# Modulation strips moved into the four rounds without routes of the PEER value product, and a new order of VectorE's work in banded attention

## What is computed

```python
mod = c_act @ mod_w[l] + mod_b[l]            # 6 vectors of 1024: shift, scale, gate, twice
sh1, sc1, g1, sh2, sc2, g2 = jnp.split(mod, 6, axis=-1)
x = x + g1 * mixer(modulate(x, norm_g[l, 0], sh1, sc1))
x = x + g2 * peer(modulate(x, norm_g[l, 1], sh2, sc2), ...)
# peer: scores -> top 16 experts e and softmax weights g for each head; then
a = gelu(einsum('pd,phkd->phk', xb, u_tab[e]))
y = einsum('phk,phkd->pd', g * a, v_tab[e])
```

## Time and profile before

| | |
|---|---|
| median of 3 runs | 2687.52 us |
| the profiled execution | 2687.45 us, its span 2685.8 us |
| TensorE matmuls busy | 2580.2 us (96%) |
| VectorE busy | 2113.9 us (79%) |
| ScalarE, GpSimd busy | 1215.1 us (45%), 461.2 us (17%) |
| mean granted TensorE clock | 0.98 |
| HBM read | 531.85 MB, 199 GB/s over the span |

### The profile page before, as it was taken

One profiled execution on the slowest core, in us unless ns is written; L12 is line 12 of the kernel. 1 busy time (PEld: TensorE's weight loads), 2 busy tenths in 40 slices (PEclk: granted clock), 3 DMA queues, 4 the chain that ended last, 5 costly groups with the idle time before them and its releaser, 6 DMA issues.

```text
span 2685.8 us, 49507 instructions
## 1 busy us (share of the span) xinstructions
PE 2580.2 (96%) x17564; PEld 2253.9 (84%) x17564; DVE 2113.9 (79%) x3580; ACT 1215.1 (45%) x1760; POOL 461.2 (17%) x365
## 2 busy tenths in 40 slices
PE   5999999999999999899999999999999999999998
PEld 4879999888877877799998888778888799767986
DVE  6787997887898768867978888998777877657754
ACT  3444444554434445444444554434445454324543
POOL 1104992000000100006990000000011000100000
PEclk8999999999999999899999999999999999999999
DMA  8655555454567877354555555567786556854454
GB/s 310 249 187 159 178 176 172 163 168 161 170 214 230 286 251 249 123 175 160 177 176 172 164 165 167 187 225 261 263 281 249 191 190 200 294 206 163 158 183 146
DMA packets 147628, 536.92 MB, mean 200 GB/s; under 512 B 16784, under 2 KB 17168, under 8 KB 147232
## 3 DMA queue, kind: packets, MB, share of 16 engines
q1 hardware_dynamic: 115088, 417.08, 46.5%
q0 software_dynamic: 31104, 113.26, 12.3%
q10 hardware_dynamic: 1296, 4.72, 0.5%
HBM read 531.85 MB, written 3.15 MB: 199 GB/s over the span
## 4 chain that ended last, share of the span: by engine, by line
PE 78%; DVE 9%; issue 4%; POOL 3%; DMA 2%; ACT 2%; DVEq 0%; ACTq 0%; SPq 0%; POOLq 0%
PE ps L1933 20%; PE ps L1504 9%; PE ps L2646 7%; PE ps L716 6%; PE ps L1478 6%; PE ps L1430 5%; PE ps L1508 5%; PE ps L2628 4%; PE ps L1482 3%; POOL split_lo L1555 3%; PE ps L1891 3%; PE ps L2632 2%; DVE split_lo L1567 2%; DMA ring<-in_stream 1%; PE ps L369 1%
## 5 line engine op out<-in xcount | busy, mean ns | idle before, releaser
L1542 ACT ACTIVATE split_hi<-ring 128x1024 fp32r<-128x1024 f32 x764 | 805.3, 1056 | 773.5 <-PE ps L1482 202.3
L1567 DVE TENSOR_TENSOR split_lo<-ring,split_hi 128x1024 fp32r<-128x1024 f32 x576 | 703.2, 1221 | 202.5 <-ACT split_hi L1542 201.9
L1555 POOL TENSOR_TENSOR split_lo<-ring,split_hi 128x1024 fp32r<-128x1024 f32 x128 | 342.7, 2695 | 155.6 <-ACT split_hi L1542 155.2
L1539 ACT ACTIVATE gate_hi<-gate 128x256 fp32r x256 | 106.9, 418 | 442.3 <-PE ps L1933 442.3
L1933 PE MATMUL ps<-split_hi,gate_hi 128*128 128x512 f32 x1024 | 285.9, 400 | 1.0 <-ACT split_hi L1542 0.5
L1933 PE MATMUL ps<-split_hi,gate_lo 128*128 128x512 f32 x1024 | 277.8, 392 | 1.8 <-DVE gate_lo L1565 1.7
L1933 PE MATMUL ps<-split_lo,gate_hi 128*128 128x512 f32 x1024 | 276.8, 391 | 0.0
L1478 PE MATMUL ps<-h_parts,split_hi 128*128 128x256 f32 x2048 | 266.8, 283 | 0.0
L1504 PE MATMUL ps<-h_parts,split_hi 128*128 128x512 f32 x1024 | 261.2, 397 | 0.0
L1478 PEld LDWEIGHTS ps<-h_parts,split_hi 128*128 128x128 f32 x2048 | 254.9, 192 | 0.0
L386 POOL DMA_DIRECT2D mod_w<-in_mod x96 | 51.0, 531 | 1141.4 <-ACT gate L1608 418.3
(11 more groups left out here) (399 smaller groups left out, 4018.3 us busy)
## 6 DMA issues: line engine op xcount, KB each, us to landing
ring<-in_stream SPq DMA_DIRECT2D x782, 512.0 KB, 4.3
mod_w<-in_mod POOLq DMA_DIRECT2D x96, 512.0 KB, 4.8
small<-in_mod POOLq DMA_DIRECT2D x80, 512.0 KB, 5.8
gate<-in_mod POOLq DMA_DIRECT2D x32, 512.0 KB, 7.0
gate<-in_mod ACTq DMA_DIRECT2D x8, 512.0 KB, 11.6
gate<-in_mod SPq DMA_DIRECT2D x8, 512.0 KB, 10.2
x_kept<-x POOLq DMA_DIRECT2D x4, 512.0 KB, 3.6
gate<-x_kept POOLq DMA_DIRECT2D x4, 512.0 KB, 8.2
```

Source lines behind the costliest of these rows:

```text
L1542: nc.scalar.activation(split_hi[:, e, :], ring[:, slot, e * D:(e + 1) * D], ACT.Copy).then_inc(hi_made, 1)
L1555: nc.gpsimd.tensor_tensor(split_lo[:, e, :], ring[:, slot, e * D:(e + 1) * D], split_hi[:, e, :].bitcast(F32), ALU.subtract).then_inc(lo_m ...
L1567: nc.vector.tensor_tensor(split_lo[:, e, :], ring[:, (START[name] + j) % RING, e * D:(e + 1) * D], split_hi[:, e, :].bitcast(F32), ALU.sub ...
```

## The change

Three parts. First, in both layers' v products the six strips are made in rounds 4 to 7 only: four slabs with two chunks each, then one slab with none, in which TensorE sums; the store is one slab later. (Every 16th slab has neither.) For that, rounds 4 to 6 are written out on VectorE and TensorE. Second, x is copied to HBM as four DMAs of 256 KB, each issued when its half is ready. Third, the order of VectorE's work in banded attention. The core of the diff:

```diff
@@ peer_score_scalar
-            a.wait_ge(x_kept, 32 * (l + 1))
+            a.wait_ge(x_kept, 64 * (l + 1))
@@
-        STRIP_CHUNKS = [[0], [1], [2], [3, 4], [5], [6], [7], []]
+        STRIP_SUMS, STRIP_STORES = (4, 9, 14, 20, 25, 30), (5, 10, 15, 21, 26, 31)
@@ routed_slab_vector
-            if odd and with_strip:
-                strip_part_vector(v, l, i, j)
@@ strip_part_vector
-            for k in STRIP_CHUNKS[j]:
-                strip_chunk_vector(v, l, i * DC - 2 * DC, k, 8 * l)
-            if j == 7:
-                strip_store_vector(v, l, i - 2)
+            q, k = divmod(8 * (i - 4) + j - (8 * (i - 4) + j) // 16, 5)
+            if 8 * (i - 4) + j in STRIP_STORES:
+                strip_store_vector(v, l, STRIP_STORES.index(8 * (i - 4) + j))
+            if (8 * (i - 4) + j) % 16 < 15 and k < 4:
+                for n in (2 * k, 2 * k + 1):
+                    strip_chunk_vector(v, l, q * DC, n, 8 * l)
@@ peer_routes_vector
-            with v.eng.Fori(4, 7) as i:
+            for i in range(4, 7):
                 for j in range(8):
                     slab(i, j)
@@ peer_out_tensor, body
-                    if j == 7 and strip:
-                        strip_sum(t, i * DC + (before - DC))
+                    if strip and 8 * (i - 4) + j in STRIP_SUMS:
+                        strip_sum(t, before + DC * (STRIP_SUMS.index(8 * (i - 4) + j) + 1))
@@
-            for i0, i1, routes, strip in ((1, 2, True, False), (2, 4, True, True), (4, 7, False, True)):
+            for i0, i1, routes, strip in ((1, 2, True, False), (2, 4, True, False)):
                 with t.eng.Fori(i0, i1) as i:
                     body(i, routes, strip)
             t.seen.clear()
+            for i in range(4, 7):
+                body(i, False, True)
@@ softmax_vector(..., ahead=4)
-            for i, part in ((0, 0), (0, 1), (1, 0), (1, 1)):
+            parts = [(0, 0), (0, 1), (1, 0), (1, 1)]
+            for i, part in parts[:ahead]:
                 logits(i, part)
                 maxima(i, part)
             probT_vector(v, at_, 0)
+            for i, part in parts[ahead:]:
+                logits(i, part)
+                maxima(i, part)
@@ swa_vector
-            row_from_col(v, "g1_1", modc[:, PLACE[MOD1[1] + G1], :], 5, "V")
             for b in range(5, 8):
                 less_splits_vector(v, "swa_q", b, b + 1)
                 side_chunks_vector(v, "swa", b - 1, b)
-            side_chunks_vector(v, "swa", 7, 9)
+            row_from_col(v, "g1_1", modc[:, PLACE[MOD1[1] + G1], :], 5, "V")
+            side_chunks_vector(v, "swa", 7, 8)
+            turned_vector(v, "swa_k", kT_s, bank=4, chunks=2)
             ... (rotation of the queries)
-            turned_vector(v, "swa_k", kT_s, bank=4, chunks=2)
             turned_vector(v, "swa_qt", qT_s, bank=4)
             softmax_vector(...
-                           [lambda: None,
+                           [lambda: side_chunks_vector(v, "swa", 8, 9),
             ...
+                           ahead=3)
@@ gpsimd
-                    pool.dma_start(io["x_kept"][:, i, :], x[:, i, :]).then_inc(x_kept, 16)
+                        pool.dma_start(io["x_kept"][:, i, half(nb)], x[:, i, half(nb)]).then_inc(x_kept, 16)
```

More of the change, by code:

```diff
@@ L415, in strip_store_vector @@
             nc.vector.tensor_tensor(
-                modc[:, bass.ds(s, 1), :].rearrange("p a n -> p (a n)"), ps_reg(7, 0, 8),
-                cols[:, bass.ds(s * 8 + COLS["mod_b"], 8)], ALU.add).then_inc(strip_stored, 1)
+                modc[:, s, :], ps_reg(7, 0, 8),
+                cols[:, s * 8 + COLS["mod_b"]:s * 8 + COLS["mod_b"] + 8], ALU.add).then_inc(strip_stored, 1)
         side_landed = [sem(f"side_landed{n}") for n in range(4)]
@@ L1811, in routes_merge_vector, with routed_slab_vector @@
                                     ALU.mult).then_inc(banks_free, 1)
-        STRIP_CHUNKS = [[0], [1], [2], [3, 4], [5], [6], [7], []]
-        def routed_slab_vector(v, name, l, i, j, first, with_strip=False):
+        STRIP_SUMS, STRIP_STORES = (4, 9, 14, 20, 25, 30), (5, 10, 15, 21, 26, 31)
+        def routed_slab_vector(v, name, l, i, j, first):
             odd = name[0] == "v"
@@ L1858, in peer_routes_vector @@
                         for j in range(8):
-                            routed_slab_vector(v, name, l, i, j, False, i0 == 2)
+                            routed_slab_vector(v, name, l, i, j, False)
                 if name[0] == "u":
@@ L2096, in build, with softmax_vector @@
         MX, NM, DEN, RD, EX = range(5)
-        def softmax_vector(v, at_, dst, scale, mask, sinks, in_waits):
+        def softmax_vector(v, at_, dst, scale, mask, sinks, in_waits, ahead=4):
             nm, H = at_.name, at_.heads
@@ L2295, in swa_vector @@
                            rows[:, ROWS["sinks"]:ROWS["sinks"] + SWA_H],
-                           [lambda: None,
+                           [lambda: side_chunks_vector(v, "swa", 8, 9),
                             lambda: side_chunks_vector(v, "swa", 9, 10),
-                            lambda: less_splits_vector(v, "swa_out", 0, 1), lambda: less_splits_vector(v, "swa_out", 1, 2)])
+                            lambda: less_splits_vector(v, "swa_out", 0, 1), lambda: less_splits_vector(v, "swa_out", 1, 2)],
+                           ahead=3)
             turned_lo_vector(v, "swa_o", yT_lo, swa_y, bank=4)
@@ L3027, in _ @@
                 pool.wait_ge(lo_free, TILE0[f"v{l}"] + 2 + (LAYER + NT * D) // SEQ)
-                pool.wait_ge(x_kept, 32 * (l + 1))
+                pool.wait_ge(x_kept, 64 * (l + 1))
                 for i in range(NT):
```

## The result

The changed kernel takes 2750.18 us (median of 4 runs, 2744.68 to 2760.40) against 2686.45 us (4 runs, 2677.56 to 2694.27) for the kernel before beside it: ratio 1.0248, 95% interval 1.0228 to 1.0268. Run again on another chip it gave 1.0198 (1.0169 to 1.0227). The forecast was 2720: the direction was right and the size was not, +33 us forecast and +64 measured (+59 between the two profiled executions, 2746.31 against 2687.45). So a difference of a few us between two traces may be nothing.

The account below looks back on a forecast made before the run. It took TensorE to bound the kernel (78% of the chain of waits), VectorE in rounds 2 and 3. Terms -18.7 + 57.6 - 3.3 + 4.8 - 7 - 0.5 = +32.9 gave 2720 us, range 2692 to 2752.

Parts of the forecast that it names:

- Term 1: v product, rounds 2 and 3, both layers: strips leave, -25.4 us; their sums come back later, +6.7; net -18.7 us.
- Term 2: v product, rounds 4 to 7: chunks wait for loads through two slots, 36 tight intervals of 7.1 us, +57.6 us.
- term 3: v product, layer 0, rounds 4 to 7: holes already there are contained in the new intervals, -3.3 us.
- rival A: v product, rounds 4 to 7: waits for loads hide and the change is faster, 2665 us; chance 0.13.
- Term 5: v product: TensorE stands before 12 sums, slower matmuls follow at lower clock; 0 to 19 us, a quarter taken, +4.8.
- Term 6: Banded attention, layer 1: queries turn sooner, TensorE's idle time before the first outputs goes; -7 us (-3 to -9).
- Term 7: Copy of x, layer 0: ScalarE's single 2.5 us wait for it; -0.5 us, between +0.5 and -1.5.
- Terms 3 and 4: v product, rounds 4 to 7: old holes contained in new intervals, -3.3 us; rounds 4 to 6 written out, 0.
- B: v product, rounds 4 to 7: second load of a pair sets the pace, 8.2 us and more; 2760 us; chance 0.15.

Follow-up runs that it names:

- strips only: Kernel before with only the strips moved into rounds 4 to 7, attention and copy of x as before: 2733.13 us, ratio 1.0222.
- four slots: The changed kernel with four load slots for strips instead of two: 2679.15 us, ratio 0.9974 to the kernel before.
- half loads: The changed kernel loading 256 KB of each chunk instead of 512 KB (results wrong, only time counts): 2695.06 us, ratio 1.0045.
- sum in the slab: The changed kernel with each strip's sum between the two tiles of its slab instead of ahead of it: 2734.05 us, ratio 1.0224.
- written out only: Kernel before with only rounds 4 to 6 of the v product written out instead of looped: 2681.78 us, ratio 0.9991.
- attention only: Kernel before with only the new banded attention order and x copied in four DMAs: 2679.07 us (0.9992), run again 2680.61 us (0.9990).
- the change, again: The same changed kernel run again on another chip: 2740.80 us, ratio 1.0198 to the kernel before.
- array kept busy: The changed kernel with ten added 128-column matmuls on constants ahead of each wait for a strip's sum: 2748.13 us, ratio 1.0236.

## Why the prediction was right in direction and wrong in size

**Term 1 (-25.4, and +6.7 for the sums): right.** The stretches above cut before the sum of round 3, so the term falls in them as -25.4 + 3.4 = -22.0 in the routed rounds and -3.4 + 6.7 = +3.4 in the plain ones. Measured: -22.2 in the first.

**Term 2 (+57.6): the right mechanism, about the right size.** With term 3 the idle time was to rise by 54; it rose by 44 in the first trace of the change and by 50.5 in the second, with intervals of 6.75 and 7.06 us where 7.1 was forecast. In the first, 26.7 us of idle time stood behind `gate_lo` and 19.6 before the sums, which the prediction had called paid by the head start of the empty slab. Landings of 512 KB took 4.8 and 5.0 us at the median and 3.4 at the least over all traces with two slots, and those of 256 KB 3.7 and 3.0. The Trainium skill, page "DMA: Bandwidth & Descriptors", section on the anatomy of one DMA, has a fit that gives an estimate of 3.2 us for 512 KB and 2.6 for 256 KB. No landing of these traces is as short as that. The prediction named what the time would be if loads were so quick (rival A) and rightly went by the rows of the kernel's own traffic.

**Term 5 (+4.8, "a quarter"): this is the step that failed.** In its place stand 36.3 us of extra busy time, of which the granted clock accounts for 28 (before: 2); the second trace has 35.1, the strips only 30.9. The prediction set the upper end at 12 slabs x 1.6 = 19 and took a quarter because sums in the old plain rounds showed nothing. But those sums had no idle time before them. The one of round 2 in layer 0 stands in a stretch with 3.3 us of it and had a slab of 7.18 behind it: that was the case to scale from. And the slab is not the only place: a sum after a long wait doubles too (3.58 us for 1.84), and some 15 of the 36.3 us lie away from the sums. What the runs showed in its place: the waits that the change makes bring slower matmuls with them. Extra busy time went from 36.3 us to 13.3 with four slots, 11.1 without loads, and 4.2 when the sum also waited for nothing, and four slots move more bytes per second than the change, so it is not the transfers that slow the matmuls. It is no simple rate: the half loads have 12.5 us idle and 19.1 extra, the sum in the slab 46.2 and 24.1.

Step by step against the profiled execution: forecast +32.9; waits (terms 2 and 3) -10.2, extra busy time (term 5) +31.5, attention +2.9, copy of x +1.6, term 1 -0.2, sum +58.5; measured +58.9.

**Term 6 (-7): too large.** In the profiles, in us from the first matmul of the key and value product; "whole" ends with the first of the output product:

| trace | attention edits | first outputs begin | they take | whole |
|---|---|---|---|---|
| before | no | +66.1 | 7.06 | 86.5 |
| strips only | no | +64.7 | 3.79 | 80.9 |
| written out only | no | +64.6 | 3.76 | 80.9 |
| the change | yes | +61.0 | 7.09 | 82.4 |
| attention only, twice | yes | +62.4, +60.8 | 7.09, 6.95 | 82.7, 82.0 |
| the change, again | yes | +64.2 | 4.71 | 83.8 |
| array kept busy | yes | +61.5 | 6.14 | 81.0 |
| five others | yes | +60.7 to +61.5 | 7.09 | 82.5 to 83.2 |

The outputs mostly start 3 to 5 us sooner, and the idle time before them falls from 6.98 us to 4.08, not to nothing:

```profile
1137.22 7.09 PE L2092 MATMUL ps<-gate 128*128 128x64 f32 x32 [4.08 <-DVE gate L2109]
```
```profile
1134.09 2.47 DVE L2172 COPY gate<-ps 128x512 f32<-128x512 f32 x4
1136.49 2.47 DVE L2109 SCALAR_TENSOR_TENSOR gate<-ps,band 128x512 f32<-128x512 f32 x4
```

The probability copies start where the forecast had them. The forecast let the outputs start 0.9 us behind that, about as before (0.8); here it is 3.1. The first outputs go into the bank of `ps` from which the first of the last logits reads (the kernel gives both bank 0), and the new order puts those logits behind all four copies: the first of them takes 0.68 us and ends at 1137.17, and TensorE starts at 1137.22. The forecast did not see this wait, and it takes 2.2 us of the gain.

The other error is the low clock, which the forecast read as a fixed 7.06 us. Two of three kernels with the old order run these 32 matmuls in under 3.8; there the low level fell on the scores and turns ahead of them (16 turns in 3.67 us instead of 2.03), beside VectorE's work on the logits, and the whole is 80.9. With the new order nine of ten run them in 6.1 to 7.1 us, and no whole is under 81.0. So the one trace of before that was there to read held an unusual case, and against the other two of the old order the new one gains nothing. This rests on one execution of each kernel; the timed runs agree (0.999, with 1 inside both intervals).

**Term 7 (-0.5): no gain.** The wait is 3.6 us, where the earlier trace rows have 2.5: +1.1. Over all traces it is 2.4 to 3.6 us with four copies and 2.5 to 3.0 with two.

```profile
ACT h_parts L1001 <- DMA x_kept<-x: 3.6, 1, 3.6
```

**Terms 3 and 4:** the old holes went into the new intervals as reckoned, and written-out loops cost nothing.

**Rivals.** A (waits hide) is refuted by the 57.7 us for which VectorE waits. B (the second load of a pair sets the pace, 8.2 us and more) came closest in time (2760), for a wrong reason: the intervals are 6.75 us. The prediction had no rival in which its own waits were right and what they do to the clock was larger; that is the one that happened. That the median of 2750 lies inside the range, which stopped at 2752, is luck: its upper end came from part of B.

## What to carry to other kernels

When work that consumes prefetched loads is bunched, compare the round trip of one slot (last use, signal, issue, landing) with the time between uses of that slot, and add slots before moving the work: two more slots turned +2.0 to +2.5% into -0.3%. Price a new wait of TensorE at more than its length: between the changed kernel and the one with four slots each us of idle time goes with some 0.6 us of slower matmuls (39.2 us less idle and 23.0 less extra busy time). And put a short dependent operation, such as a one-column sum, in the middle of a slab and not where its input is just being finished: with four slots that took the extra busy time from 13.3 to 4.2 us; with two, where the loads set the pace, it gained nothing. Finally, before a reader is moved in an engine's order, look which bank it frees, and for whom: the first outputs of attention waited for logits that the new order had put behind the copies.

## What the runs showed of the hardware

Landings of 512 KB are longer when more of them are under way (6.0 us at the median and up to 11.2 with four slots, 4.8 and 7.3 with two, layer 0), while the total rate rises, from 255 to 296 and 300 GB/s: more in flight buys rate with latency. The lower clock level reached short stretches that nobody would call idle. In the kernel before, the sum of round 3 in layer 0 begins without a wait, the 24 route matmuls ahead of it having waited 0.29 us, and the eight matmuls behind it take 1.97 and 1.89 us for four instead of 1.07:

```profile
844.88 0.87 PE L1891 MATMUL ps<-small 128*128 128x64 bf16 x24 [0.29 <-DVE small L1799]
845.59 1.93 PE L369 MATMUL ps<-ones,mod_acc 128*128 128x1 f32 x16
847.38 1.97 PE L1933 MATMUL ps<-split_hi,gate_hi 128*128 128x512 f32 x4
849.14 1.89 PE L1933 MATMUL ps<-split_hi,gate_lo 128*128 128x512 f32 x4
```

In layer 1 of the same trace the two such sums are followed by twelve matmuls at full pace (2.83 us). Waits of 0.2 to 0.3 us before a sum went either way in the kernel with four slots: behind six of ten the next twelve matmuls took 4.4 us, behind the other four 2.9. Why some such sums draw the low level and others don't stays open.
